# Spread gates leave their banks by ScalarE and are added and multiplied on GpSimd, three quarters of four

## Time and profile before

| | |
|---|---|
| median of 3 runs | 3780.98 us |
| profiled execution, whole | 3775.98 us |
| its span, first to last instruction | 3773.8 us |
| mean granted clock of TensorE over the span | 0.973 |
| busy PE, DVE, ACT, POOL | 3616.3, 3027.5, 2047.2, 133.2 us |
| bytes moved, mean rate | 744.51 MB, 197 GB/s |

### The profile page before, as it was taken

How to read it: one execution, slowest core, us unless ns; L and a number is a source line. 1 busy time by engine, 2 the same in 40 slices (tenths; PEclk the granted TensorE clock), 3 DMA queues, 4 the chain that set the end, 5 groups by cost and what they waited for, 6 DMA issues and landing times. The chain is left out here.

```text
span 3773.8 us, 59656 instructions
## 1 busy us (share of the span) xinstructions
PE 3616.3 (96%) x22322; PEld 3106.1 (82%) x22322; DVE 3027.5 (80%) x6276; ACT 2047.2 (54%) x4310; POOL 133.2 (4%) x128
## 2 busy tenths in 40 slices
PE   6999999999899979999999999999999999999898
PEld 5887688888788758998888887899988888888787
DVE  7887688887588776988888956589798997789766
ACT  3554555655355545545665456454565654555555
POOL 0000000000000001400000000050000000000000
PEclk9999999999889989999999999899999999999999
DMA  8767376766257514444454454244455545686354
GB/s 328 276 249 290 107 299 224 284 246 242 101 220 268 200 66 158 178 158 179 179 180 182 164 191 156 90 171 166 169 179 184 179 173 179 224 306 267 135 191 155
DMA packets 119617, 744.51 MB, mean 197 GB/s; under 512 B 13857, under 2 KB 14273, under 8 KB 44833
## 3 DMA queue, kind: packets, MB, share of 16 engines
q1 hardware_dynamic: 118082, 737.57, 53.4%
q10 hardware_dynamic: 416, 2.07, 0.1%
q0 software_dynamic: 832, 1.06, 0.1%
HBM read 738.54 MB, written 1.05 MB: 196 GB/s over the span
## 5 line engine op out<-in xcount | busy, mean ns | idle before, releaser
L216 PE MATMUL bank<-h_split,weights_high 128*128 128x512 f32 (+1 forms) x5824 | 1715.0, 358 | 14.2 <-DVE h_split L734 8.3
L1127 ACT ACTIVATE weights_high<-weight_ring 128x512 fp32r<-128x512 f32 x2248 | 1292.2, 623 | 657.4 <-PE bank L216 376.3
L1135 DVE TENSOR_TENSOR weights_low<-weight_ring,weights_high 128x512 fp32r<-128x512 f32 x2168 | 1396.4, 688 | 276.2 <-ACT weights_high L1127 254.4
L216 PE MATMUL bank<-h_split,weights_low 128*128 128x256 f32 x4800 | 1268.9, 280 | 0.0
L216 PEld LDWEIGHTS bank<-h_split,weights_high 128*128 128x128 f32 x5824 | 1014.8, 190 | 161.4 <-issue 14.7
L216 PEld LDWEIGHTS bank<-h_split,weights_low 128*128 128x128 f32 x4800 | 911.0, 190 | 38.3 <-issue 0.8
L216 PE MATMUL acc<-weights_high,hidden_high 128*128 128x512 f32 x1552 | 613.1, 395 | 2.6 <-DVE hidden_low L1309 2.4
L216 PE MATMUL acc<-weights_low,hidden_high 128*128 128x512 f32 x1552 | 604.9, 390 | 0.0
L216 PE MATMUL acc<-weights_high,hidden_low 128*128 128x512 f32 x1552 | 604.7, 390 | 0.0
L216 PEld LDWEIGHTS acc<-weights_high,hidden_low 128*128 128x128 f32 x1552 | 291.4, 188 | 63.1
L216 PEld LDWEIGHTS acc<-weights_low,hidden_high 128*128 128x128 f32 x1552 | 291.6, 188 | 59.6 <-issue 0.2
(11 more groups left out here) (352 smaller groups left out, 3441.0 us busy)
## 6 DMA issues: line engine op xcount, KB each, us to landing
weight_ring<-stream SPq DMA_DIRECT2D x574, 1024.0 KB, 4.8
h_feat<-slots SPq DMA_DIRECT2D x96, 512.0 KB, 5.9
h_tok<-slots SPq DMA_DIRECT2D x94, 512.0 KB, 6.0
work<-slots SPq DMA_DIRECT2D x26, 512.0 KB, 8.3
mod_sums<-biases SPq DMA_DIRECT2D x7, 1536.0 KB
h_feat<-rows SPq DMA_DIRECT2D x8, 512.0 KB, 3.8
work<-rows SPq DMA_DIRECT2D x7, 512.0 KB, 4.8
work<-biases SPq DMA_DIRECT2D x1, 1536.0 KB
```

Source lines behind the costliest of these rows:

```text
L216: ins = self.nc.tensor.matmul(out, lhs, rhs, start=start, stop=stop)
L1127: act.activation(k.w_hi[:, b, q * self.QUARTER:(q + 1) * self.QUARTER], self.raw(g, q), ACT.Copy).then_inc(k.highs_ready, 1)
L1135: return eng.tensor_tensor(k.w_lo[:, b, w], self.raw(g, q), k.w_hi[:, b, w].bitcast(F32), ALU.subtract)
```

## The change

`BESIDE` becomes quarters 1, 2 and 3. In these, ScalarE copies each of the two banks whole (two instructions of 512 columns, scaled by 1/32768) into the two halves of `k.gate`, which frees the bank; it waits first until the additions of the batch before have read that buffer (`pieces_added`). GpSimd adds the two pieces of each buffer (two instructions of 256 columns) into one of two `whole` tiles, laid out with the 16 tokens next to each other, and multiplies `hidden` by it (512 columns, both inputs in SBUF). ScalarE waits for this last multiply (`sums_gated`) ahead of the quarter's out halves. VectorE keeps the builds and quarter 0's multiply, and loses the additions and multiplies of the other three.

```diff
--- before.py
+++ after.py
@@ -141,8 +141,8 @@
         self.rests_made = ctx.enter_context(nc.semaphore("weighted_lows_made"))
         self.onehots_made = ctx.enter_context(nc.semaphore("onehots_made"))
         self.gate_banks = ctx.enter_context(nc.semaphore("gate_banks_filled"))
-        self.seconds_out = ctx.enter_context(nc.semaphore("second_pieces_out"))
-        self.quarters_gated = ctx.enter_context(nc.semaphore("quarters_gated"))
+        self.pieces_added = ctx.enter_context(nc.semaphore("gate_pieces_added"))
+        self.sums_gated = ctx.enter_context(nc.semaphore("gated_by_pool"))
         self.gated = ctx.enter_context(nc.semaphore("hidden_gated"))
         self.heads_normed = ctx.enter_context(nc.semaphore("heads_normed"))
         self.heads_gated_early = ctx.enter_context(nc.semaphore("heads_gated_by_pool"))
@@ -2010,14 +2010,14 @@
     WIDEN_AT = 15
     EXP_AT = 23
     TURN_AFTER = 33
-    BESIDE = (1, 2)
+    BESIDE = (1, 2, 3)
 
     def __init__(self, k, route, found, hidden, gate, rest, places, pairs, pieces, hot1, hot2, mask, whole,
-                 second):
+                 both):
         super().__init__(k)
         self.route, self.found, self.hidden = route, found, hidden
         self.gate, self.rest, self.places, self.pairs, self.pieces = gate, rest, places, pairs, pieces
-        self.hot1, self.hot2, self.mask, self.whole, self.second = hot1, hot2, mask, whole, second
+        self.hot1, self.hot2, self.mask, self.whole, self.both = hot1, hot2, mask, whole, both
         route.host = self
         self.halves = expert_order()
         self.take_halves(len(self.halves))
@@ -2036,7 +2036,8 @@
                 g = begin + b * (end - begin) // (BATCHES - 1)
                 self.build_at[g].append((q, b))
                 self.spread_after[g].append((q, b))
-                self.gate_at[g + 3].append((q, b))
+                if q not in self.BESIDE:
+                    self.gate_at[g + 3].append((q, b))
 
     def count_lows(self):
         k = self.k
@@ -2161,6 +2162,9 @@
         k = self.k
         for g in range(self.ahead, self.POOL_HALVES):
             self.early_low(pool, g)
+        for q in self.BESIDE:
+            for b in range(BATCHES):
+                self.multiply_sums(pool, q, b)
 
     def scalar(self, act):
         k = self.k
@@ -2171,13 +2175,13 @@
                 c = self.halves[g + 1][1]
                 if c % QUARTER == 0:
                     if c // QUARTER in self.BESIDE:
-                        act.wait_ge(k.quarters_gated, self.number * len(self.BESIDE) + 1 + self.BESIDE.index(c // QUARTER))
+                        act.wait_ge(k.sums_gated, self.sums_through(c // QUARTER, BATCHES - 1))
                     else:
                         act.wait_ge(k.gated, self.units_through[c // QUARTER, BATCHES - 1])
                 act.activation(self.top(c), self.place(c), ACT.Copy).then_inc(k.tops_made, 1)
             for q, batch in self.spread_after[g - 3]:
                 if q in self.BESIDE:
-                    self.take_seconds(act, q, batch)
+                    self.take_both(act, q, batch)
             if self.WIDEN_AT <= g < self.WIDEN_AT + 8:
                 self.route.widen(act, g - self.WIDEN_AT)
             if g == self.EXP_AT:
@@ -2220,18 +2224,29 @@
                 self.build(dve, q, batch)
             self.sum_step(dve, g)
 
-    def seconds_through(self, q, b):
-        return 2 * (BATCHES * (self.number * len(self.BESIDE) + self.BESIDE.index(q)) + b + 1)
-
-    def take_seconds(self, act, q, b):
-        k = self.k
+    def sums_through(self, q, b):
+        return BATCHES * (self.number * len(self.BESIDE) + self.BESIDE.index(q)) + b + 1
+
+    def take_both(self, act, q, b):
+        k, done = self.k, 2 * self.sums_through(q, b)
         for i, (t, n, bank, free, units, through) in enumerate(self.fills[q, b]):
             act.wait_ge(k.gate_banks, through)
-            if q != self.BESIDE[0] or b > 0:
-                act.wait_ge(k.gated, self.fills[self.batch_before(q, b, 1)][i][5])
-            act.activation(self.second[:, t:t + n, :],
-                           k.bank[:, bank, :].rearrange("p (t i n) -> p i t n", t=n, i=PIECES)[:, 1],
-                           ACT.Copy).then_inc(k.seconds_out, 1)
+            if done > 2:
+                act.wait_ge(k.pieces_added, done - 3 + i)
+            act.activation(self.both[i], k.bank[:, bank, :], ACT.Copy, scale=1.0 / GATE_SCALE).then_inc(k.gated, units)
+
+    def multiply_sums(self, pool, q, b):
+        k, done, whole = self.k, 2 * self.sums_through(q, b), self.whole[b % 2]
+        for i, (t, n, bank, free, units, through) in enumerate(self.fills[q, b]):
+            pool.wait_ge(k.gated, through)
+            pieces = self.both[i].rearrange("p (t i n) -> p i n t", t=n, i=PIECES)
+            pool.tensor_tensor(whole[:, :, t:t + n], pieces[:, 0], pieces[:, 1], ALU.add).then_inc(k.pieces_added, 1)
+        if b == 0:
+            pool.wait_ge(k.hidden_made, self.chunks_before() + (q + 1) * QUARTER)
+        pool.wait_ge(k.pieces_added, done)
+        first = q * QUARTER % PLACES
+        hidden = self.hidden[:, first:first + QUARTER, b * BATCH:(b + 1) * BATCH]
+        pool.tensor_tensor(hidden, hidden, whole, ALU.mult).then_inc(k.sums_gated, 1)
 
     def split_gates(self, dve):
         k = self.k
@@ -2277,27 +2292,13 @@
 
     def multiply(self, dve, q, b):
         k = self.k
-        first = q * QUARTER % PLACES
-        for t, n, bank, free, units, through in self.fills[q, b]:
-            dve.wait_ge(k.gate_banks, through)
-            if q in self.BESIDE:
-                pieces = k.bank[:, bank, :].rearrange("p (t i n) -> p i t n", t=n, i=PIECES)
-                dve.wait_ge(k.seconds_out, self.seconds_through(q, b) + (t > 0) - 1)
-                dve.tensor_tensor(self.whole[:, t:t + n, :], pieces[:, 0], self.second[:, t:t + n, :],
-                                  ALU.add).then_inc(k.gated, units)
+        dve.wait_ge(k.gate_banks, self.units_through[q, b])
         if b == 0:
             dve.wait_ge(k.hidden_made, self.chunks_before() + (q + 1) * QUARTER)
+        first = q * QUARTER % PLACES
         hidden = self.hidden[:, first:first + QUARTER, b * BATCH:(b + 1) * BATCH]
-        if q in self.BESIDE:
-            dve.wait_ge(k.gated, self.units_through[q, b])
-            gates = self.whole.rearrange("p t n -> p n t")
-        else:
-            gates = k.bank[:, 2 + b % 2, :].rearrange("p (t i) -> p i t", t=BATCH)
-        ins = dve.scalar_tensor_tensor(hidden, gates, 1.0 / GATE_SCALE, hidden, ALU.mult, ALU.mult)
-        if q not in self.BESIDE:
-            ins.then_inc(k.gated, 2)
-        elif b == BATCHES - 1:
-            ins.then_inc(k.quarters_gated, 1)
+        dve.scalar_tensor_tensor(hidden, k.bank[:, 2 + b % 2, :].rearrange("p (t i) -> p i t", t=BATCH),
+                                 1.0 / GATE_SCALE, hidden, ALU.mult, ALU.mult).then_inc(k.gated, 2)
 
 
 
@@ -3494,7 +3495,8 @@
     room, early = Room(k), Room(k)
     hidden = room(PLACES, S)
     hot1 = [halfwords(room(PIECES * QUARTER * BATCH // 2), PIECES * BATCH, QUARTER, dt=F16) for _ in range(2)]
-    whole, second = room(BATCH, QUARTER), room(BATCH, QUARTER)
+    whole = [room(QUARTER, BATCH) for _ in range(2)]
+    both = [k.gate[:, i * BANK:(i + 1) * BANK] for i in range(2)]
     mask = [halfwords(room(QUARTER * BATCH // 2), BATCH, QUARTER, dt=F16) for _ in range(2)]
     pairs, pieces = halfwords(room(2 * S), 2 * S, 2, dt=F16), halfwords(room(PIECES * S), PIECES * S, 2, dt=F16)
     tok, feat = k.h_tok.rearrange("p a b -> p (a b)"), k.h_t.rearrange("p a b -> p (a b)")
@@ -3511,7 +3513,7 @@
     return [Boundary(k, "add", False, NORM_AT["p0" if layer == 0 else "p1"], None),
             ToFeatureRows(k, q_t, 2 * PEER_HEADS), KeyScores(k, q_t, scores),
             Experts(k, route, found, hidden, gate, rest, places, pairs, pieces, hot1, hot2, mask,
-                    whole, second)]
+                    whole, both)]
 
 
 def fox_rows(I):
```

## The result

The changed kernel takes 3838.68 us (median of 4, 3830.31 to 3839.52) against 3779.2 us (4 runs of the kernel before beside it): 1.0148 times, 95% interval 1.0101 to 1.0196. The forecast was 3840 us. The profiled execution has a span of 3837.1 us, 63.3 more than before.

What follows compares the result with a forecast made beforehand. TensorE was taken as the bound, with VectorE equally full in quarter 3. Profiled 3776 + 54 (quarter 3) + 4 (quarters 1 and 2) = 3834, 5 more against the median: 3840 us; range 3785 to 3895, forecast's own 3820 to 3865.

Steps and rivals of the forecast that it cites:

- The bound: Expert stages: TensorE busy throughout; VectorE equally full only in quarter 3, 78.2 of 79.28 us, against 148.1 of 164.3 in quarter 1.
- The sum for them: Quarters 1 and 2: VectorE 148.1 - 11.2 - 16.9 + 41.3 = 161.3 us against 164.3, costing 1 us per stretch.
- Exclusion of the two engines: GpSimd's time adds to VectorE's two-SBUF-input work: 41.3 us per stretch, +54 us in quarter 3 of both stages.
- the rival: No turn-taking: quarter 3's one-hot builds and weight lows pass beside GpSimd, 3766 us; chance 0.15.
- 0.13 us per instruction: Time recovered per GpSimd operation beside VectorE; recovering nothing would add 6 us to each stretch's GpSimd term.
- the sum: Cost over the profiled execution: +54 us in quarter 3 of both stages and +4 us in quarters 1 and 2.
- 2.5 us of lead: Quarter 3: VectorE may begin a low some 2.5 us ahead of TensorE's need, absorbing that much once.
- TensorE's saving: Quarter 3: 16 wider products replace 32, saving 0.47 us per group, 15 us over both stages, lost while waiting for lows.
- What I said would show it: Quarter 3: 105 us, TensorE waiting for weight lows, lows 1 us or more, GpSimd additions near 1; quarter 1: VectorE near 160.
- my own conditions for being wrong: Lows keeping 690 ns beside GpSimd, quarter 3's stretch under 79 us, or TensorE waiting mostly for onehots or banks.
- The wait chain: Rival in quarter 3: products wait for ScalarE's copies, these for GpSimd's additions; adds 48 us, 3888 us; chance 0.22.

Runs made afterwards that it cites:

- memset run: Changed kernel with GpSimd's three instructions per batch replaced by memsets about as long, which read nothing (additions and gating left out): 3751.9 us, 0.9951.
- copy runs: Changed kernel with GpSimd's three instructions per batch replaced by one-input copies of 512 columns (additions and gating left out): 3783.6 us, 1.0032.
- e2: Kernel before with quarter 3 in the 64-column form too, additions and multiplies on VectorE, nothing on GpSimd: 3800.6 us, 1.0065.
- e4: Changed kernel with ScalarE writing banks out as piece, column, token, so GpSimd's additions read packed inputs: 3803.9 us, 1.0079.
- e9: Changed kernel with GpSimd's instructions on 8 of 32 keys' columns and four outgoing buffers in place of two: 3780.8 us, 1.0010.
- two-quarter kernels: Changed kernel with quarters 1 and 2 alone on ScalarE and GpSimd: 3763.7 us, 0.9983; the same with packed additions: 3763.2 us, 0.9974.
- e3: Changed kernel with four outgoing buffers in place of two, ScalarE waiting for additions of two batches before: 3830.6 us, 1.0158.
- e5: Changed kernel with GpSimd's three instructions per batch on 8 of 32 keys' columns, all waits kept: 3773.5 us, 1.0010.
- e6: Changed kernel with both packed additions and four outgoing buffers: 3802.3 us, 1.0083.
- e7: The memset run: changed kernel with GpSimd's three instructions per batch replaced by memsets: 3751.9 us, 0.9951.
- e10: Changed kernel with GpSimd's three instructions per batch replaced by three one-input copies of 512 columns: 3783.6 us, 1.0032.
- better version: Changed kernel with quarters 1 and 2 alone on ScalarE and GpSimd, and packed additions: 3763.2 us, 0.9974 times the kernel before.

## Why the prediction was right

**The bound.** Right. Quarter 3 was the one place where VectorE was as full as TensorE, and the whole loss lies there. Quarters 1 and 2 took GpSimd's work and even gave 0.47 us each instead of costing 1. The sum for them was too high: it put VectorE at 161.3 us, and quarter 1's row has 145.9. In the memset run, where GpSimd disturbs nobody, VectorE is busy 123.8 us in that stretch, so GpSimd's reads add 22 us there and not 41.3; the rest of GpSimd's time falls where VectorE waits or reads a bank.

**Exclusion of the two engines.** Right, and the step that carried the forecast. The exclusion was read from products of 5 and 6 columns and from fp32 additions; the rival hung on whether builds and weight lows behave the same, and they do (1229 to 1654 ns, 695 to 870 ns). SBUF — State Buffer of the Trainium skill (Who interferes with whom) has it as an exclusive lock for GpSimd instructions that read SBUF, not for those that only write; the memset and the copy runs agree (74.4 and 90.5 us). The page says that the loser "fully blocks", by which nothing is recovered; I had kept 0.13 us per instruction by the earlier trace rows. The traces speak for a small recovery: in the change GpSimd's own time is 15 x 3.37 = 50.6 us, VectorE was stretched by 32.8 and idle for 9.5, so at least 8 us of GpSimd's 45 instructions, 0.18 us each, ran beside a VectorE that was neither held up nor idle. The same sum gives 0.08 us each with a quarter of the columns and four buffers (18.5 - 5.6 - 9.1). How much of this is only how the records of neighbouring instructions overlap stays open.

**Sizes.** That 3840 meets 3838.7 us so closely is luck. The profiled executions differ by 63 us where the sum had 58, and within quarter 3, which grew by 32.5 us per stage and not by 27.2, larger errors cancelled. VectorE's own work is 69.4 us, not 67.7. GpSimd stretches it by 32.8 us, not by 41.3, although an addition takes 1.05 us at least and not 0.94. And VectorE then stands idle for 9.5 us, mostly for weight highs, where the sum had no idle time and took 2.5 us of lead off. In all that is 111.7 against 106.5. Quarters 1 and 2 were to cost 4 us and gave 1.9. The medians differ by 59.5 us and the profiled executions by 62.9, since the kernel before was profiled in an execution 3 us under its median, and that brought the absolute figures together.

**TensorE's saving.** Over-estimated: the forecast had 0.47 us per group; in the memset run quarter 3's gaps of one and two halves are 3.33 and 6.05 us instead of 3.65 and 6.38, so a group of 16 products takes 0.61 us there and saves 0.33. The 0.45 came from quarter 1, whose gaps of three and four halves mix halves of both kinds. It made no difference, as the saving was lost in either case.

**What I said would show it.** Partly wrong. I expected TensorE to wait for weight lows and said that waits for one-hots and banks would speak against me. They are what the trace has (13.6, 11.9 and 10.4 us against 2.0 for lows). The lows' mean was to be 1 us or more and is 0.87, GpSimd's additions near 1 us have a mean of 2.3 in the stretch, and VectorE in quarter 1 was to be near 160 us and is 145.9. So the trace met one of my own conditions for being wrong, while the memset run shows that the cause was right. It was the inference from cause to wait that failed, as the order in the code explains: in VectorE's stream a build stands between two lows, TensorE takes the one-hots of a batch ahead of the next half, and so a late VectorE is seen first at the one-hots. No run tests this explanation.

**The wait chain.** It exists (ScalarE stands 27.6 us per stretch) and was a rival with 0.22. Four buffers removed 10 us of that wait and 3.8 us of the stretch, and no run removed it all while GpSimd still read SBUF. With VectorE busy 102.2 of 111.6 us the chain can hold 9.5 us of the stretch at most, 4.5 more than the memset run has; the rest is exclusion.

## What to carry to other kernels

Before work is handed to an idle GpSimd, add its time to VectorE's over the stretch concerned, and count every GpSimd instruction that reads SBUF beside every VectorE one with two SBUF inputs. Here, where the sum stayed under the bounding engine's time, the move was free (VectorE's 123.8 us, less 11.8 that read a bank, and GpSimd's 50.6 are 162.6 us in a stretch of 163.8), and where it went over, nearly all of what stood over was paid (112 us against 79). The share of busy time over a kernel does not show this; the stretch where two engines are full does. And a long wait in the trace is not the loss: split the stretch into busy and idle time of the engine that should be full, and ask how much of the idle time the wait could hold.

## What the runs showed that was not expected

*An instruction of GpSimd can starve.* The exclusion is not fair: with VectorE's stream full, one addition of 256 columns took 11.1 us (14.3 in the run with four buffers, 15.5 with packed additions too), until VectorE ran out of work. With two quarters alone the longest, without packing, was 5.2 us.

*Some 10 us lie elsewhere and come and go.* From the last spread of one expert stage to the first of the next the kernel before took 430.2 us, the change 428.2, `e2` 429.9, `e4` 430.7 and `e9` 428.4. But it was 416.6 and 420.0 us in the two-quarter kernels, 420.9 in `e3`, 419.2 in `e5`, 419.7 in `e6`, 417.9 in `e7` and 419.1 in `e10`, with the same instructions in it. So the short form is not bound to two quarters. The stretch 200 to 220 us after the last spread, in the kernel before and in the better version:

```profile
2365.59:2385.59 20.00, 18.19 (x119) 17.55 (x118) 7.93 (x20) 5.09 (x10) 0.00 (x0) 0.76 0.00 1
```

```profile
2364.04:2384.04 20.00, 18.37 (x151) 17.99 (x150) 9.90 (x21) 6.72 (x12) 0.00 (x0) 0.92 0.01 1
```

TensorE was granted 0.76 of its clock in one and 0.92 in the other, where it had just gone through a part in which hardly any weights move. These two executions differ by 10.0 us in their spans and by 10.2 in this interval. Beside each other, 11 of 12 executions of the better version took under 3770 us, and 6 of 29 of the kernel before; that these six had the short form too is a guess. What makes the shorter form likelier no run here tells: it stays open, and the 0.3% of the better version should be read with that.
